# One core, a hybrid encoder layer: the inverse's join and the low-rank rounds rewritten for 64x64 tiles of the matmul array

## The reference, cut to what matters

```python
w = jnp.exp(-RWKV_DECAY_SCALE * jax.nn.sigmoid(
    rwkv_w0.astype(f32) + jnp.tanh(wd) @ rwkv_w_up.astype(f32)))
a = jax.nn.sigmoid(rwkv_a0.astype(f32) + ad @ rwkv_a_up.astype(f32))
...
def step(s, inp):
    r_t, w_t, k_t, v_t, kk_t, a_t = inp
    sa = jnp.einsum('bhij,bhj->bhi', s, -kk_t)
    s = (s * w_t[:, :, None, :] + sa[..., None] * (kk_t * a_t)[:, :, None, :]
         + v_t[..., None] * k_t[:, :, None, :])
    y = jnp.einsum('bhij,bhj->bhi', s, r_t)
    return s, y
```

## Time and profile before

| | us |
|---|---|
| median of 3 runs | 2328.3 |
| lowest and highest | 2328.03, 2329.17 |
| span of the profiled execution | 2324.5 |
| PE busy in it | 2247.6 (97%) |
| DVE busy | 1445.6 (62%) |
| ACT busy | 1280.4 (55%) |
| POOL busy | 577.6 (25%) |

### The profile page before, as it was taken

The page is one execution under the profiler, slowest core; times in us unless marked ns, Lnnn a source line. Parts: engine busy times, 40 slices in busy tenths (PEclk is TensorE's granted clock), DMA queues, the critical chain, the costliest instruction groups (busy, mean ns, idle before and its releaser), DMA issues. The chain is left out here.

```text
span 2324.5 us, 72365 instructions
## 1 busy us (share of the span) xinstructions
PE 2247.6 (97%) x31109; PEld 1702.3 (73%) x31109; DVE 1445.6 (62%) x2699; ACT 1280.4 (55%) x2757; POOL 577.6 (25%) x1070
## 2 busy tenths in 40 slices
PE   7999999999999999889999999999999998899998
PEld 5777777777777777777888888888888885444443
DVE  6344544454455554567777777777777777457675
ACT  8355555555555545645666666666666664343333
POOL 0000000000000000355455555455555565000000
PEclk9999999999999999999999999999999999999999
DMA  7112222222333321222222333222223234666675
GB/s 244 69 56 70 79 79 88 79 79 79 102 114 115 108 100 45 57 57 69 69 78 77 82 87 86 78 69 71 78 82 87 84 87 140 203 211 211 224 234 183
DMA packets 217278, 244.62 MB, mean 105 GB/s; under 512 B 110080, under 2 KB 159552, under 8 KB 212608
## 3 DMA queue, kind: packets, MB, share of 16 engines
q1 hardware_dynamic: 211056, 217.44, 30.6%
q10 hardware_dynamic: 5904, 22.55, 2.6%
HBM read 141.83 MB, written 98.10 MB: 103 GB/s over the span
## 5 line engine op out<-in xcount | busy, mean ns | idle before, releaser
L2111 PE MATMUL first<-h,w_hi 128*128 128x256 f16 (+1 forms) x2496 | 419.7, 273 | 0.0
L2070 POOL TENSOR_TENSOR r_inv_tmp<-r_inv 64x30 f32<-64x30 f32 (+14 forms) x480 | 265.2, 552 | 418.2 <-DMA r_inv<-scratch_blocks 381.9
L748 PE MATMUL d<-h,w_hi 128*128 128x256 f16 (+1 forms) x2176 | 350.4, 270 | 0.0
L2111 PE MATMUL first<-h,w_lo 128*128 128x256 f16 (+1 forms) x1248 | 338.5, 272 | 0.0
L748 PE MATMUL d<-h,w_lo 128*128 128x256 f16 (+1 forms) x1088 | 290.1, 269 | 0.0
L2072 POOL TENSOR_TENSOR r_inv<-r_inv,r_inv_tmp 64x30 f32<-64x30 f32 (+14 forms) x480 | 279.9, 583 | 37.6
L2111 PEld LDWEIGHTS first<-h,w_hi 128*128 128x128 f16 x2496 | 238.2, 98 | 50.3 <-issue 18.8
L748 PEld LDWEIGHTS d<-h,w_hi 128*128 128x128 f16 x2176 | 208.9, 98 | 32.8 <-issue 3.5
L2013 POOL MEMSET r_run_s<- 128x128 f16 x1 | 0.2, 204 | 923.9 <-POOLq L390 923.9
L748 PE MATMUL first<-h,w_hi 128*128 128x256 f16 (+1 forms) x1168 | 184.5, 268 | 5.0 <-DVE w_lo L1236 3.1
L2111 PE MATMUL r_d<-h,w_hi 128*128 128x256 f16 (+1 forms) x960 | 159.2, 272 | 0.8 <-DVE carry_s L2742 0.8
(11 more groups left out here) (393 smaller groups left out, 5118.0 us busy)
## 6 DMA issues: line engine op xcount, KB each, us to landing
h<-in_x SPq DMA_DIRECT2D x33, 512.0 KB, 3.9
r_ops<-in_x SPq DMA_DIRECT2D x33, 512.0 KB, 4.0
out_y<-r_ops SPq DMA_DIRECT2D x33, 512.0 KB, 7.7
scratch_hT<-h SPq DMA_DIRECT2D x16, 1024.0 KB, 7.1
h<-scratch_hT ACTq DMA_DIRECT2D x15, 1024.0 KB, 6.8
scratch_mg<-m_hl SPq DMA_DIRECT2D x33, 256.0 KB, 2.0
r_zr<-scratch_zr SPq DMA_DIRECT2D x33, 256.0 KB, 3.8
r_bon<-scratch_bonus SPq DMA_DIRECT2D x33, 256.0 KB, 5.7
```

Of the source, the lines that this page charges most:

```text
L748: mm = pe.matmul(out, lhs(k, a, w), rhs(k, a, w), start=(n == 0), stop=(n == len(terms) - 1))
L2070: step(pool.tensor_tensor(tmp, inv[0:n, 0:u, u:u + 1].to_broadcast([n, u, w]), inv[0:n, u:u + 1, u + 1:32].to_broadcast([n, u, w]), ALU.mult))
L2111: mm = pe.matmul(out, lhs(k, a, w), rhs(k, a, w), start=(m == 0), stop=(m == 3 * KT - 1))
```

## The change

* The join becomes a product of 64*64 tiles: the stationary operand is 64 rows of `Wt_all` and 64 of its columns (the 32 wanted ones first, whatever follows behind them; `Wt_all` has 160 columns so that the last window fits), the moving one the same 32 columns of `TT` over all 64 rows, the output all 64 partitions of the half. Rows 0 to 31 of each half of `Wt` must then be zero, so `keep_w` becomes a multiplication by a column of zeros and ones, `low_rows`. Head 0 stays on partitions 0 to 63 for input and output, head 1 on 64 to 127: the eight matmuls use two of the four tiles, those on the diagonal.
* Each rank matmul of 64*128 becomes two of 64*64: 24 matmuls a rank, on all four tiles.
* POOL's set-up gets four more memsets, and `SET_ALL` is 40. No instruction changes its place.

```diff
-SET_SUMS, SET_ALL = 15, 36
+SET_SUMS, SET_ALL = 15, 40
...
-        Wt = sb("Wt", [P, 2, 2, 32])
+        Wt_all = sb("Wt", [P, 160])
+        low_rows = sb("low_rows", [P, 1])
...
+        Wt = Wt_all[:, 0:128].rearrange("p (a g t) -> p a g t", a=2, g=2)
...
+                done(pool.memset(Wt_all[:, :], 0.0))
+                done(pool.memset(low_rows[:, :], 0.0))
+                for h in range(2):
+                    done(pool.memset(low_rows[64 * h + 32:64 * h + 64, :], 1.0))
...
                         for rows, (out, m) in parts:
-                            mm = pe.matmul(out[:, g * n:(g + 1) * n], up[rows, w, (g0 + g) * P:(g0 + g + 1) * P],
-                                           lor[rows, a, 0:n], start=(i == 0), stop=(i == 2))
+                            for h in range(2):
+                                c0 = (g0 + g) * P + CH * h
+                                mm = pe.matmul(out[hrows(h), g * n:(g + 1) * n], up[rows, w, c0:c0 + CH],
+                                               lor[rows, a, 0:n], start=(i == 0), stop=(i == 2))
...
                 for g in range(4):
                     for h in range(2):
-                        r0 = 64 * h
-                        mm = pe.matmul(AB[r0:r0 + 32, 1, 256 + g * 32:256 + (g + 1) * 32], Wt[r0 + 32:r0 + 64, swapped(h, g), g // 2, :],
-                                       TT[r0 + 32:r0 + 64, b % 2, ch, g, 32:64], start=True, stop=True,
-                                       tile_position=(r0 + 32, r0))
+                        c0 = 64 * swapped(h, g) + 32 * (g // 2)
+                        mm = pe.matmul(AB[hrows(h), 1, 256 + g * 32:256 + (g + 1) * 32], Wt_all[hrows(h), c0:c0 + CH],
+                                       TT[hrows(h), b % 2, ch, g, 32:64], start=True, stop=True)
...
-                dve.tensor_copy(Wt[:, :, :, :], pairs(EO, 384, 32)).then_inc(*w_ok.up(q))
+                dve.tensor_scalar(Wt, pairs(EO, 384, 32), low_rows[:, 0:1], None, ALU.mult).then_inc(*w_ok.up(q))
```

## The result

The changed kernel takes 2338.6 us (median of 6 runs, 2330.2 to 2340.2), the kernel before 2327.9 us on the same chip (6 runs, 2325.2 to 2329.2). The ratio is 1.0043, with a 95% interval of 1.0030 to 1.0056. The forecast was 2331.6 us, with a range to 2334.5. The time went up by 10.7 us where 3.3 were forecast: the direction of the forecast was right, and two thirds of the loss were not in its sum. A run's time stands 1.7 or 1.8 us above its span, so the profiled execution of the kernel before was one of some 2326.3 us, on the low side, and that of the changed kernel one of 2340.2, on the high side: they differ by 14.0 us where the medians differ by 10.7.

A forecast was written before the change was run, and what follows sets the result against it. PE was taken to bound the middle of the second stage, busy 198.57 of 200 us. Sixty counted joins at +0.055 us gave +3.3, the ranks 0, on a median of 2328.3: 2331.6 us, range 2327.5 to 2334.5.

The forecast's parts named there:

- The join, +0.055 each: From solve to the next piece: 0.77 us against 0.715, eight rounds at 0.058; 60 counted joins give +3.3 us.
- faster rival: At the join: the 32 moving columns set the step, 0.61 us a join, -6.3 us, 2322.0 us; chance 0.10.
- slower rival: At the join: loads never run ahead, 0.80 us a join, +5.1 us, 2333.4 us; chance 0.14.
- The ranks' rounds and edges: At lwa0 and lwa2: still six rounds of 0.11; 0.10 saved at lwa0 becomes waiting at lwa2, so 0 us.
- The rival that both changes of size are saved: At the ranks: lwa2's wait is not last in most passes, +3.3 - 2.8 = +0.5, 2328.8 us; chance 0.12.
- `keep_w`, POOL's set-up, the layout: On DVE and POOL: keep_w hidden, under 1 us in all without cover; POOL's four memsets fit in 8.7 us.
- The 48 more PE instructions of a pass cost nothing while a round takes 0.11: On PE's queue at the ranks: the additional instructions of each pass add no time.
- The bounds of the ranks' term: For the 14 rank passes: between 0 and 14 x 0.2 = 2.8 us less.
- unless PE soon meets a wait that another engine ends: In the second stage's middle: PE's gains or losses are the kernel's, except under this condition; no size given.

The follow-up runs named there:

- e14: e9 with the new join, so all edits of the change, at e9's instruction positions: 2323.2 us, ratio 0.9977.
- e9: Kernel before with new 64*64 ranks, old join, and 124 idle waits a pass (5 in pass 1), 2816 PE instructions a pass: 2319.8 us, ratio 0.9956.
- e1: Changed kernel with the rank lines of before, so the new join without the new ranks: 2331.9 us, ratio 1.0016.
- e3: Kernel before with only the larger Wt tile (160 columns) and one unused column behind it: 2327.5 us, ratio 0.9993.
- e6: Kernel before with 172 idle waits a pass (106 in pass 1), 2816 PE instructions a pass: 2325.7 us, ratio 0.9995.
- e7: As e6, kernel before with 172 idle waits a pass, but 195 in pass 1: 2346.3 us, ratio 1.0075.
- e11: As e9, new ranks and old join with 124 idle waits a pass, but 226 in pass 1: 2335.5 us, ratio 1.0027.
- e8: Changed kernel with 124 idle waits a pass (1 in pass 1), 2816 PE instructions a pass: 2324.0 us, ratio 0.9988.
- e2: Kernel before with only the ranks changed to 64*64, old join: 2340.6 us, ratio 1.0056.
- e10: Kernel before with 48 idle waits a pass in the pieces ahead of lwa0 and behind lwa2: 2341.9 us, ratio 1.0053.
- e5: Kernel before with 48 more idle instructions a pass, spread over the projection's 39 pieces: 2333.3 us, ratio 1.0020.
- e13: e9 with the old ranks, their 48 fewer instructions a pass made up by idle waits beside them: 2340.6 us, ratio 1.0053.
- e4: The changed kernel again, unaltered, for a second profile and time: 2338.6 us, ratio 1.0049.

## Why the prediction failed, point by point

* **The join, +0.055 each: right.** The step is 0.059 us, the first one short, the way out 0.15, `solve` 0.23. 66 joins at 0.056 are 3.7 us; e14 lies 3.4 to 4.9 above e9, and e1 measured 4.1. The faster rival (steps of 0.032) falls, and so does the slower rival (0.80 a join): solve to piece is 0.78. The load that the prediction takes from the Trainium skill, "TensorE: Matmul & The Clock Gate", section "LDWEIGHTS (loading the stationary operand)", an estimated 0.053, is below the measured step of 0.059.
* **The ranks' rounds and edges: right.** Rounds as before, 0.08 us saved at the edge of `lwa0`, and all of it swallowed by the wait of `lwa2` for the carry, as forecast; the fastest pass is unchanged (61.56 in e9, 61.55 before). The rival that both changes of size are saved falls.
* **`keep_w`, POOL's set-up, the layout: right**, as far as e1 and e3 can tell.
* **"The 48 more PE instructions of a pass cost nothing while a round takes 0.11": this step failed.** It asked whether PE can issue them in time, and it can. It did not ask where the code comes from. The bounds of the ranks' term, 0 and 2.8 us less, had no cost side at all, and nothing else in the range made up for that. The count moved the code transfers from a rhythm of threes to one of twos: the two waits for the round trip grew by 5.4 us (7.7 against 2.3), and the stops for code by 0.4 (2.2 against 1.8; the table's row of 1.3 at L2319 is a stop at 1061.86, which belongs to the work ahead of the window), beside the join's 3.1 in that window of 56 joins. These are 8.9 us, against 9.3 by which the work between 1062 and 1925 us grew. The other 4.7 of the profile's 14.0 lie outside: 2.4 ahead of it (0.8 in the first stage, which the edit does not touch, and 1.3 that stop) and 2.3 behind it, where PE stood still for 2.98 us and the clock was low.
* **Views that would have shown it.** The earlier trace rows gave PE busy for 97% and left 3%, 77 us. The queue of kind "instruction" stands on the same page and was not read; the two "issue" rows at L2179 in the kernel before (1.0 and 0.8 us, in the middle of a group) are not in the prediction either. The prediction named the condition, "unless PE soon meets a wait that another engine ends", and gave it no price. The chain that ends such a wait has next to no slack: in its fastest passes (53.3 us) DVE comes to `TD` without idle time, and of the 4.4 us that pass 10 takes beyond, 3.76 are DVE's wait and 1.96 PE's. In passes 7 and 11 (54.3 and 54.6) DVE had no wait: there it came late itself.

What is shown: the place of the code transfers, set by the number of PE instructions, moves this kernel with old ranks and old join between 2325.7 and 2346.3 us (e6, e7), and with new ranks between 2319.8 and 2335.5 (e9, e11), with no change in its work. The changed kernel itself is 14.6 us faster with nothing but idle instructions added (e8). How the loss divides between the round trip, the stops and the lower clock is read from one trace of each kernel and was not tested one by one. What stays open: why the new ranks alone (e2, +12.8) cost some 5 us more than equal counts without them (e10, +12.0, of which 4.2 are its own waits). The traces do not settle it. They show where both lose against the changed kernel and e5: pass 2 took 70.65 us in e2 and 70.94 in e10, where it took 65.16 before, 67.55 after the change and 67.45 in e5, with a stop in `turn` of 2.55 and 2.27 us (0.22 in the changed kernel, at the same record) and the lower clock behind it. Why that stop is so different in length is not known. That the tiles cost this by themselves is unlikely, since e9 has them and is the fastest of all, and since its fastest pass is that of before; the positions within the pass differ by up to 24 instructions. The run that was to settle it, e13, did not.

## What to carry to other kernels

In a fully unrolled program whose PE is near its limit, an edit that changes the number of PE instructions in the steady loop moves every code transfer behind it. Before a few tenths of a per cent are put down to an edit, divide the loop's instructions by 256 and compare the remainders, and look whether a latency-bound chain of small transfers or a dense run of small matmuls meets a transfer of the instruction queue. Two kernels are compared more fairly at equal remainders, as e9 and e14, though even there the stops differed; and a count that makes the loop a whole number of blocks, at a place clear of both, was worth 10 us (before against e9, on one chip) to 15 us (after against e8 and e14) here; which place that is has to be tried, since e7 and e11 are whole blocks too and are the slow ones. Look at the granted clock too, in stretches of a few us around each long stop: the page's forty slices of 58 us did not show it.

## What the runs showed of the hardware that was not expected

* Two diagonal 64*64 tiles step as four do: the new join takes 388 ns from its first start to its last, 16 records, so a pair steps by 0.059 us with 32 moving columns as with 64. In these fp32 groups the step goes by the columns of the stationary operand.
* PE's code came in packets of 16 KB, one for 256 instructions, and was usable some 2.4 us (2.2 to 2.9) after its transfer began. It was not always fetched far ahead: the stop at 1944.71 lasted 2.98 us, so its transfer began 0.58 us after PE had already stopped.
* One 16 KB packet on one of 16 DMA engines went with four 64 KB stores of small packets that lasted 1.2 to 2.1 us longer (3.37 us against 4.6 to 5.5). In the pass looked at packet by packet, a sixteenth of the last store started as that packet ended.
* A satisfied wait of its own on PE's queue (51 ns) was free at one behind about every second matmul of 0.11 us (e6, 172 a pass), cost 0.30 us for 24 in three pieces (e10), and 1.35 us where some gaps held four waits (e13).
* Behind some stops and waits of PE the granted clock was 0.50 for some microseconds (e2, e4, e5, e7, e10, and the changed kernel at 1943.40). After one such stop, e7's pass 5 lost 2.7 us more.
* Undisturbed passes repeat to 0.01 us: 61.54 or 61.55 in four traces with old ranks and old join. I read the scatter of a kernel's runs (e7: 27 us from lowest to highest, e9: 7) as how often its transfers collide, but did not measure that. The traces show one other source: the first stage is the same code in all sixteen, and the first strict block behind it ended between 950.7 and 957.4 us. From 20 to 100 us the granted clock was 0.96 in the nine traces in which it ended by 951.9, and 0.89 to 0.94 in the seven others.
